# A stick-breaking attention phase on one core: the weighted values issued ahead of the scores in each step

## What is computed

```python
def stick_breaking(q, k, v, q_pos, k_pos):
    z = jnp.einsum('bqhd,bshd->bhqs', q, k).astype(jnp.float32) * (d ** -0.5)
    causal = (k_pos[None, :] < q_pos[:, None])[None, None]
    log_beta = jax.nn.log_sigmoid(z)
    log_rest = jnp.where(causal, jax.nn.log_sigmoid(-z), 0.0)
    suffix = lax.cumsum(log_rest, axis=3, reverse=True) - log_rest
    A = jnp.where(causal, jnp.exp(log_beta + suffix), 0.0)
    return jnp.einsum('bhqs,bshd->bqhd', A.astype(v.dtype), v)
```

## Time and profile before

| | before |
|---|---|
| median of 3 runs | 3098.61 us (3094.63 to 3100.53) |
| profiled execution | 3091.68 us, span 3090.0 us |
| TensorE matmuls busy | 2896.4 us, 94% |
| VectorE busy | 1513.3 us, 49% |
| GpSimd busy | 1147.8 us, 37% |
| ScalarE busy | 1004.6 us, 33% |
| mean granted TensorE clock | 0.975 |

### The profile page before, as it was taken

The page is one execution under the profiler, slowest core; times in us unless marked ns, Lnnn a source line. Parts: engine busy times, 40 slices in busy tenths (PEclk is TensorE's granted clock), DMA queues, the critical chain, the costliest instruction groups (busy, mean ns, idle before and its releaser), DMA issues. The chain is left out here.

```text
span 3090.0 us, 50524 instructions
## 1 busy us (share of the span) xinstructions
PE 2896.4 (94%) x20331; PEld 2384.9 (77%) x20331; DVE 1513.3 (49%) x2135; ACT 1004.6 (33%) x1843; POOL 1147.8 (37%) x1001
## 2 busy tenths in 40 slices
PE   6899999999989999989998999899988996999798
PEld 5788888888877888867776777677766776877686
DVE  7232221100004777666766676567657774333333
ACT  6441211111113444434443444334435662000221
POOL 4242331111104445445544545345535563433100
PEclk9899999999999999999999999999998998999899
DMA  6543332212216554665466545754448348444443
GB/s 215 178 154 114 131 123 68 79 68 71 73 66 215 171 162 156 223 214 176 159 215 217 185 159 175 240 189 159 150 153 229 126 128 238 165 169 163 163 143 109
DMA packets 383015, 485.98 MB, mean 157 GB/s; under 512 B 27888, under 2 KB 241904, under 8 KB 382416
## 3 DMA queue, kind: packets, MB, share of 16 engines
q1 hardware_dynamic: 341200, 359.32, 36.9%
q0 software_dynamic: 34688, 111.05, 9.6%
q10 hardware_dynamic: 6912, 12.59, 1.2%
HBM read 359.28 MB, written 123.60 MB: 156 GB/s over the span
## 5 line engine op out<-in xcount | busy, mean ns | idle before, releaser
L376 PE MATMUL prj_bank<-hidden_hi,w_hi 128*128 128x512 f32 (+2 forms) x1360 | 490.9, 361 | 13.1 <-DVE w_lo L439 13.1
L378 PE MATMUL prj_bank<-hidden_hi,w_lo 128*128 128x512 f32 (+2 forms) x1360 | 487.1, 358 | 0.0
L377 PE MATMUL prj_bank<-hidden_lo,w_hi 128*128 128x512 f32 (+2 forms) x1360 | 486.8, 358 | 0.0
L1100 POOL TENSOR_TENSOR stk_beta<-stk_beta,stk_left 128x1024 f32<-128x1024 f32 (+4 forms) x160 | 275.8, 1724 | 549.2 <-DVE stk_left L1017 549.2
L809 PE MATMUL stk_g_bank<-hidden_hi,w_hi 128*128 128x512 f32 (+2 forms) x928 | 351.1, 378 | 14.6 <-PEq L62 10.8
L811 PE MATMUL stk_g_bank<-hidden_hi,w_lo 128*128 128x512 f32 (+2 forms) x928 | 336.6, 363 | 0.0
L810 PE MATMUL stk_g_bank<-hidden_lo,w_hi 128*128 128x512 f32 (+2 forms) x928 | 335.8, 362 | 0.0
L376 PEld LDWEIGHTS prj_bank<-hidden_hi,w_hi 128*128 128x128 f32 x1360 | 256.9, 189 | 44.8 <-DVE w_lo L439 13.3
L378 PEld LDWEIGHTS prj_bank<-hidden_hi,w_lo 128*128 128x128 f32 x1360 | 256.7, 189 | 32.5
L377 PEld LDWEIGHTS prj_bank<-hidden_lo,w_hi 128*128 128x128 f32 x1360 | 257.0, 189 | 31.3
L1017 DVE TENSOR_TENSOR_SCAN stk_left<-stk_rest,stk_left 128x513 f32<-128x513 f32 x192 | 244.6, 1314 | 8.1 <-ACT stk_rest L965 8.0
(11 more groups left out here) (254 smaller groups left out, 5460.2 us busy)
## 6 DMA issues: line engine op xcount, KB each, us to landing
stk_kd<-in_cache_sb_k SPq DMA_DIRECT2D x64, 1024.0 KB, 5.4
stk_vd<-in_cache_sb_v SPq DMA_DIRECT2D x64, 1024.0 KB, 7.3
w_raw<-in_w_in SPq DMA_DIRECT2D x112, 512.0 KB, 3.8
scratch_zT<-stk_g_out POOLq DMA_DIRECT2D x72, 256.0 KB, 2.3
mrg_gate<-scratch_zT SPq DMA_DIRECT2D x24, 768.0 KB, 4.4
scratch_zT<-prj_z POOLq DMA_DIRECT2D x48, 256.0 KB, 2.3
prj_w<-in_w_in SPq DMA_DIRECT2D x18, 512.0 KB, 3.9
mrg_u_raw<-scratch_uT SPq DMA_DIRECT2D x9, 1024.0 KB, 9.2
```

The lines of the kernel that those rows point to most:

```text
L376: pe.matmul(out, w_hi[u][:, k, :], hi[:, k, :], start=k == 0, stop=False)
L377: pe.matmul(out, w_hi[u][:, k, :], lo[:, k, :], start=False, stop=False)
L378: last = pe.matmul(out, w_lo[u][:, k, :], hi[:, k, :], start=False, stop=k == KC - 1)
L1100: pool.tensor_tensor(bt, bt, left[prompts.index(n) % 2][:, :, 1:keys + 1], ALU.mult).then_inc(a_done, 1)
```

## The change

In TensorE's loop over the steps of the stick phase the values of unit s - 5 are issued ahead of the scores of unit s instead of behind them. All waits stay inside the two functions, and all other engines keep their order.

```diff
@@ -915,10 +915,10 @@
             turn_k(0, 0)
             turn_k(0, 1)
             for s in range(N + LAG_O):
+                if s >= LAG_O:
+                    add_o(s - LAG_O)
                 if s < N:
                     scores(s)
-                if s >= LAG_O:
-                    add_o(s - LAG_O)
                 turn_k(s + 1, 0)
                 gates_part(s, 0)
                 if 0 <= s - LAG_T < N:
```

## The result

The changed kernel takes **3123.56 us** (median of 7 runs, 3112.17 to 3133.42); the kernel before took 3098.70 us in the 7 runs beside it (3094.63 to 3104.34). The ratio is 1.0072, with a 95% interval of 1.0055 to 1.0089: slower by some 17 to 28 us, and far above the range I had given (3090 to 3111). What came is rival 2 in the main, a little dearer than I had priced it.

The account below looks back on a forecast made before the run. TensorE's in-order issue was taken to bound the stick phase. Terms of -10.0, +15, -0.2 and -3.9 us summed to +0.9, about +1 on the median of 3098.6: 3099.6 us, range 3090 to 3111.

Parts of the forecast that it names:

- rival 2: Stick phase: scores no longer cover VectorE's late sum, and later scans run into GpSimd's subtraction; +20 us, 3119; chance 0.23.
- What bounds the kernel: Stick phase: TensorE's in-order issue sets the length; only instruction spacing and waits in its order can change it.
- (a): TensorE's neighbouring blocks: 67 steps that open a tile save one change of array shape, 0.15 us each, -10.0 us.
- (c): Scores issued later: values fill nine gaps before scores that need copied turned keys, -3.9 us; later sigmoids cost nothing.
- (b): Values issued earlier: they wait for VectorE's late sum in 21 steps, 0.7 us in the mean, +15 us; bounds +9 to +22.
- step 92: Late-sum example: values' wait of 0.77 us would become 1.2, not 1.96, because VectorE's chain starts earlier too.
- step 86: Late-sum example: values moved to the scores' start at 1431.92 wait about 1.0 us where they had not waited.
- Small terms: Earlier copies out of turn_bank -1.2, earlier value loads -0.5, shape gains lost ahead of VectorE waits +1.5; together -0.2 us.
- The first reload: First reload of the hidden rows: swap changes little; values can't fill the scores' 3.93 us wait for ScalarE.
- (2): Sign: value blocks' waits on VectorE rise from about 6 to about 20 us; forecast wrong under 12 or past 30.

Follow-up runs that it names:

- pair with short scans: Running products cut to 16 columns (output wrong) in the kernel before and in the changed kernel: 3075.59 us in the old order, 3063.50 in the new.

## Why the prediction was wrong, point by point

**What bounds the kernel: right.** TensorE's in-order issue, with gaps; all of the change is in the gaps and the neighbours.

**(a) Neighbours, -10 us: right.** Mask to turn is 0.056 us (forecast 0.04 to 0.06), values to scores 0.202 (0.20), turns to values 0.203. Eight turns behind a mask take 0.80 to 0.97 us where they took 0.85 to 1.02 behind values. So an opening step gains 0.09 + 0.05 = 0.14 us; I had written 0.15 for the same sum, and 67 steps make 9.4 us and not 10.0. In the pair with short scans the time without waits falls by 9.1 us, with part of (c) in it. In the changed kernel itself one sees -5.0, and 51.2 us at the 1.2 GHz level against 37.5. If all of the added 13.7 us were TensorE's issue at half speed, that is 6.9 us more, and -5.0 becomes about -12, near (a) with the part of (c) that isn't a wait. This is an estimate, and no run held the clock fixed. The granted clock fell with it, from 0.975 to 0.971 in the profiled executions.

**(c) Scores later, -3.9 us: right in its gain, wrong in its price.** The waits of L867 went from 2.8 us to 0 and the last turned keys to scores gap is filled. But "ScalarE's sigmoids start up to 1.1 us later, they have room" was read against ScalarE's next work and TensorE's next need alone. What stood behind the sigmoid, which came 0.62 us later in the nine places, was a scan with less than 0.05 us to spare against GpSimd.

**(b) Values earlier, +15 us: this is the step that failed.** It sized the late sums too small, and the price of later sigmoids on VectorE's scans, put at nothing in (c), came due here. The values' waits in their measured parts:

| | us |
|---|---|
| 21 steps, late by VectorE's chain alone (24.7 now, 5.2 before) | +19.6 |
| six steps behind a lost scan | +11.3 |
| first reload: 6.47 at the values, of which 3.93 had stood at the scores | +6.5 |
| waits for value loads (3.9 now, 1.4 before) and two steps at the end | +2.6 |
| sum (read from block starts above: 40.1) | +40.0 |

The first row is 0.9 us a step where I had taken 0.7, nearer the upper bound of 22 than +15. I had let VectorE's earlier start give back part of it on the strength of one example, step 92, and just that one came out at 2.06 us, against 1.2. Where nothing leads the chain but VectorE itself the reading was good: step 86, forecast 1.0 us, shows

```profile
1437.58 0.26 DVE L1041 TENSOR_TENSOR stk_od<-stk_o_bank,stk_od 128x128 f32<-128x128 f32 x1
...
1437.89 1.09 PE L898 MATMUL stk_o_bank<-stk_a_t,stk_v_rows 128*64 128x128 f32 x16 [0.94 <-DVE stk_od L1041]
```

The second row was not in the sum at all. Rival 2 had the mechanism in outline, and even the count, "six scans more at 2.0 us each": nine scans were lost, six of them cost a wait, 1.9 us each. But it spoke of scans that start later and into the subtraction, as its example did, 0.19 us behind it; the nine lost ones still start 0.53 us ahead. It priced the whole at +20 us, and +24.9 came. What I had against it was that a subtraction is issued in 94 of 232 steps only and that VectorE has a quarter of its time free. Neither bears on it: a chance of meeting is no argument when the order is fixed, and the rows could have been read one by one. In the trace of before, each scan that ended short beside a long subtraction (2.88 us and not 2.37) was a meeting won; the nine with the smallest lead, 0.56 us, stood apart from the next at 0.64.

Against the forecast of +0.9 us the phase came out 24 us longer. Of that 11.3 us are the lost scans, 4.6 the late steps, 3.1 the value loads with the steps at the end (+2.6 against -0.5) and 0.8 the first reload; another 4.6 is time without waits, which fell by 5.0 where the sum had 9.6.

**Small terms: -2.5 us** for L881 (forecast -1.2), 1.0 of it at the first reload, and the value loads were waited for longer and not shorter (3.9 us against 1.4). The wait of 3.5 us for a key load at step 114 is new: 3.5 in both profiles of the changed kernel, 3.3 in the new order with short scans, and 0.5 to 2.1 us in the other experiments, with either order. What sets it stays open.

**The first reload: right.** The waits there were 0.99 + 3.93 + 3.07 us at turns, scores and turned keys; now they are 6.47 at the values and 2.03 at the turned keys, with 0.29 between: 8.8 against 8.0.

**The forecast's own sign** was "wrong if (2) passes 30 us": it came to 43.8.

## What to carry to other kernels

Before a block is moved, find each VectorE instruction with two SBUF inputs that lies beside a GpSimd one and read its lead: a scan of 1.27 us beside a subtraction that took 2.88 instead of 2.37 has won a meeting that a few hundredths of a microsecond can turn into 3.99 us, and no count of free time on VectorE protects it. Take the lead that is needed from the kernel's own rows, won and lost: 0.53 us was too little here, and 0.20 was enough once four small writes stood ahead of the subtraction. Then take the price of a late take-over as the full cover that is removed, unless the thing which leads its chain moves too. If a reorder costs more than its waits explain, compare the mean of each group of instructions before and after, same count and same form: 1838 against 2225 ns was the quickest sign here.

## What the hardware showed

- Of a scan and a subtraction that start close together, the one recorded first didn't always go first. Without writes ahead of the subtraction the scan went first with a lead of 0.56 us and above (26 of before, 17 of after) and second with 0.53 and below (19 and 28). With four writes of two columns there it went first at 0.20 us and above (28 in the new order, 31 in the old) and second at 0.13 and below (17 and 14). Why a lead is needed and why it changes, the traces don't show.
- The loser stands still for as long as the winner works: a lost scan ends 1.1 us behind the subtraction's recorded end, about its whole own time of 1.27 us, even where its record starts 0.53 us ahead.
- A write of eight columns on GpSimd (0.12 us) ahead of each subtraction turned nine such meetings and 13 to 19 us of the kernel; four writes turned three meetings more and gained no time.
- Sigmoids that came 0.62 us later moved nine scans by 0.04 us, and that group of VectorE's instructions was busy for 24.8 us more, with not an instruction added.
